# The inner X levels of a blocked triangular inversion: PSUM transposes of Y in place of a second set of small products

## The reference, cut to what matters

```
def _wkv7_step(S, inp):
    r, w, k, v, kk, a = inp
    sa = jnp.einsum('bhvk,bhk->bhv', S, kk)
    S = S * w[:, :, None, :] - sa[..., None] * (kk * a)[:, :, None, :] + v[..., None] * k[:, :, None, :]
    y = jnp.einsum('bhvk,bhk->bhv', S, r)
    return S, y
```

## Time and profile before

| | |
|---|---|
| runs | 2608.56, 2600.13, 2608.91 us; median 2608.56 |
| profiled execution | span 2600.0 us from first to last instruction; no whole time of its own is listed beside it |
| PE busy over the span | 2505.0 us (96%) |
| DVE, ACT busy over the span | 1998.4 us (77%), 1537.2 us (59%) |
| scan, 562 to 796 us | 234 us of the span (9%) |
| mean granted TensorE clock | 0.979 of 2.4 GHz |

### The profile page before, as it was taken

The page is one execution under the profiler, slowest core; times in us unless marked ns, Lnnn a source line. Parts: engine busy times, 40 slices in busy tenths (PEclk is TensorE's granted clock), DMA queues, the critical chain, the costliest instruction groups (busy, mean ns, idle before and its releaser), DMA issues.

```text
span 2600.0 us, 54588 instructions
## 1 busy us (share of the span) xinstructions
PE 2505.0 (96%) x23472; PEld 2331.7 (90%) x23472; DVE 1998.4 (77%) x3066; ACT 1537.2 (59%) x2510; POOL 51.9 (2%) x57
## 2 busy tenths in 40 slices
PE   8999999989999999999999999999898899999999
PEld 8779998868887899999999999999897799998999
DVE  5555547775544799999999999999877788675884
ACT  4435434464432677777777777777666566564663
POOL 0001100000000000000000000000003000000000
PEclk9999999978999999999999999999999999998999
DMA  6223452300003599999999999999732255541453
GB/s 246 73 74 122 178 190 100 107 1 4 20 4 115 206 376 337 367 340 368 341 366 335 372 337 370 335 373 345 287 139 105 78 192 191 188 173 50 171 181 128
DMA packets 83257, 538.46 MB, mean 207 GB/s; under 512 B 9488, under 2 KB 9616, under 8 KB 38976
## 3 DMA queue, kind: packets, MB, share of 16 engines
q1 hardware_dynamic: 82368, 530.68, 55.2%
q0 software_dynamic: 640, 4.22, 0.4%
HBM read 533.81 MB, written 1.05 MB: 206 GB/s over the span
## 4 chain that ended last, share of the span: by engine, by line
PE 87%; DVE 7%; ACT 4%; issue 1%; DMA 1%; DVEq 0%; SPq 0%; PEldq 0%; ACTq 0%
PE ps L576 23%; PE ps L577 23%; PE ps L578 23%; PE ps L1469 2%; DVE sl L534 2%; PE ps L591 1%; PE ps L582 1%; PE ps L2000 1%; PE ps L1463 1%; PE ps L1447 1%; PE ps L1454 1%; DMA ring<-ws_d 1%; PE ps L2145 1%; PE ps L1425 1%; PE ps L819 1%
## 5 line engine op out<-in xcount | busy, mean ns | idle before, releaser
L2227 DVE TENSOR_TENSOR sl<-ring,sh 128x1024 fp32r<-128x1024 f32 x613 | 718.1, 1219 | 13.5 <-ACT sh L2185 10.6
L2185 ACT ACTIVATE sh<-ring 128x1024 fp32r<-128x1024 f32 x613 | 609.0, 1061 | 1.3 <-DVE xl L2070 1.3
L576 PE MATMUL ps<-sh,xh 128*128 128x256 f32 (+2 forms) x2012 | 568.0, 282 | 2.1 <-DVE sl L534 1.2
L578 PE MATMUL ps<-sh,xl 128*128 128x256 f32 (+2 forms) x2012 | 567.5, 282 | 0.0
L577 PE MATMUL ps<-sl,xh 128*128 128x256 f32 (+2 forms) x2012 | 567.0, 282 | 0.0
L576 PE MATMUL ps<-xh,sh 128*128 128x256 f32 (+2 forms) x1856 | 538.5, 290 | 22.8 <-DVE sl L534 12.7
L577 PE MATMUL ps<-xl,sh 128*128 128x256 f32 (+2 forms) x1856 | 531.2, 286 | 0.0
L578 PE MATMUL ps<-xh,sl 128*128 128x256 f32 (+2 forms) x1856 | 529.0, 285 | 0.0
L534 DVE TENSOR_TENSOR sl<-ring,sh 128x1024 fp32r<-128x1024 f32 (+1 forms) x341 | 401.0, 1201 | 74.6 <-ACT sh L527 74.3
L527 ACT ACTIVATE sh<-ring 128x1024 fp32r<-128x1024 f32 (+1 forms) x341 | 338.8, 1021 | 111.2 <-PE ps L578 102.8
L576 PEld LDWEIGHTS ps<-sh,xh 128*128 128x128 f32 x2012 | 377.8, 188 | 11.8 <-DVE sl L534 1.6
(11 more groups left out here) (555 smaller groups left out, 3861.1 us busy)
## 6 DMA issues: line engine op xcount, KB each, us to landing
ring<-ws_d SPq DMA_DIRECT2D x229, 1024.0 KB, 7.2
ring<-ws_d SPq DMA_DIRECT2D x80, 1536.0 KB, 6.4
ring<-ws_d SPq DMA_DIRECT2D x225, 512.0 KB, 6.5
ring<-ws_d SPq DMA_DIRECT2D x24, 1408.0 KB, 6.0
ring<-ws_d SPq DMA_DIRECT2D x4, 1256.0 KB, 5.4
ring<-ws_d SPq DMA_DIRECT2D x2, 1088.0 KB, 5.0
scan_t<-scn_d POOLq DMA_DIRECT2D x1, 1844.0 KB, 7.5
ring<-ws_d SPq DMA_DIRECT2D x1, 1248.0 KB, 5.6
```

The source lines that it names most:

```text
L576: e.matmul(out, ah, bh, start=start, stop=False)
L578: return e.matmul(out, al, bh, start=False, stop=stop)
L2185: e.activation(out, raw(u)[:, a:z], ACT.Copy).then_inc(*af.on("high", u, i))
L2227: e.tensor_tensor(l, raw(u)[:, a:z], f32(h), SUB).then_inc(s_fd if i < 2 else s_fp, 1)
```

## The change

The change is that X of the levels 1 to 4 (1 and 2 in the small chunk) is no longer made by 16 products of its own. After T of the next level PE turns the whole of Y with four transposes of 128x128 into one PSUM bank, and DVE copies that bank, 128x512, over X. Y of every level and X of the last level stay products. For the transposes to give X in place, the slots of the heads in Y and X are renumbered.

```
         def g_slot(i, p):
             return 8 * (i // 2 % 2) + 4 * p + 2 * (i // 4) + i % 2
 
+        def x_slot(i):
+            return 2 * (i % 4) + i // 4
+
         def y_slot(i, p):
-            return 4 * p + i % 4
+            return 2 * (i % 4) + p
...
                         last.then_inc(*pe.on("T", *u, lv))
+                        if lv > 1:
+                            b, free = psum.take(("X turn", *u, lv - 1))
+                            w.wait_ge(*free)
+                            for k in range(4):
+                                last = tr(e, PS[:, b, 128 * k:128 * k + 128], d.Y[:, 2 * k:2 * k + 2, :].rearrange("q i t -> q (i t)"))
+                            last.then_inc(*pe.on("X turn", *u, lv - 1))
                         yield
                         w.wait_ge(ac["T", *u, lv], dv["X", *u, lv - 1])
                         if lv < levels(cn) - 1:
...
-                        b, free = psum.take(("X", *u, lv), 2)
-                        w.wait_ge(*free)
-                        for i, p in HEADS:
-                            last = e.matmul(spread(PS[own(p), b:b + 2, :], lv)[:, i], d.T[own(p, cn), i, :], side(d.X[own(p, cn), i, :], lv, d.x_side), start=True, stop=True)
-                        last.then_inc(*pe.on("X", *u, lv))
+                        else:
+                            b, free = psum.take(("X", *u, lv), 2)
+                            w.wait_ge(*free)
+                            for i, p in HEADS:
+                                last = e.matmul(spread(PS[own(p), b:b + 2, :], lv)[:, x_slot(i)], d.T[own(p, cn), i, :], side(d.X[own(p, cn), x_slot(i), :], lv, d.x_side), start=True, stop=True)
+                            last.then_inc(*pe.on("X", *u, lv))
...
                     for lv in range(1, levels(cn)):
+                        if lv > 1:
+                            w.wait_ge(pe["X turn", *u, lv - 1])
+                            e.tensor_copy(d.X.rearrange("q i t -> q (i t)"), PS[:, psum["X turn", *u, lv - 1], :]).then_inc(*dv.on("X", *u, lv - 1))
+                            psum.gone["X turn", *u, lv - 1] = [dv.now()]
                         yield
                         if lv < levels(cn) - 1:
                             b = psum["Y", *u, lv]
                             w.wait_ge(pe["Y", *u, lv])
-                            e.copy_predicated(side(d.Y, lv, d.y_side), level_mask(d.y_level, lv, d.y_side), spread(PS[:, b:b + 2, :], lv)).then_inc(*dv.on("Y", *u, lv))
+                            by_slot = PS[:, b:b + 2, :].rearrange("q p (i t) -> q i p t", i=4)[:, :, :, 0:32]
+                            e.copy_predicated(side(d.Y, lv, d.y_side), level_mask(d.y_level, lv, d.y_side), by_slot).then_inc(*dv.on("Y", *u, lv))
                             psum.gone["Y", *u, lv] = [dv.now()]
-                        w.wait_ge(pe["X", *u, lv])
+                        else:
+                            w.wait_ge(pe["X", *u, lv])
```

More of the change, by code:

```diff
@@ L1462, in steps @@
                             for i, p in HEADS:
-                                last = e.matmul(spread(PS[part(0, i), b:b + 2, :], lv)[:, y_slot(i, p)], d.X[own(p, cn), i, :],
+                                last = e.matmul(spread(PS[part(0, i), b:b + 2, :], lv)[:, 4 * p + i % 4], d.X[own(p, cn), x_slot(i), :],
                                                 side(d.T[own(p, cn), i, :], lv, d.y_side), start=True, stop=True)
                             last.then_inc(*pe.on("Y", *u, lv))
-                        b, free = psum.take(("X", *u, lv), 2)
-                        w.wait_ge(*free)
-                        for i, p in HEADS:
-                            last = e.matmul(spread(PS[own(p), b:b + 2, :], lv)[:, i], d.T[own(p, cn), i, :], side(d.X[own(p, cn), i, :], lv, d.x_side), start=True, stop=True)
-                        last.then_inc(*pe.on("X", *u, lv))
+                        else:
[4 more added lines that the diff above has]
+                            last.then_inc(*pe.on("X", *u, lv))
                         yield
@@ L1488, in steps @@
                     for i, p in HEADS:
-                        last = e.matmul(PS[part(0, i), b + p, col(i)], d.X[own(p, cn), i, :], d.Z[own(p, cn), i, :], start=True, stop=True)
+                        last = e.matmul(PS[part(0, i), b + p, col(i)], d.X[own(p, cn), x_slot(i), :], d.Z[own(p, cn), i, :], start=True, stop=True)
                     last.then_inc(*pe.on("N", *u))
@@ L1712, in steps @@
                     m = sn(f"{d.y_level}0")[:, 0:cn].bitcast(u32)
[L1713 removed]
+                    e.copy_predicated(d.Y[:, :, 0:cn].rearrange("q (i p) t -> q p i t", p=2), m[:, None, None, :].broadcast_to([128, 2, 4, cn]), eights(b, cn)).then_inc(*dv.on("Y", *u, 0))
                     psum.gone["Ut", *u] = [dv.now()]
@@ L1719, in steps @@
                             k = g_slot(4 * x, p)
-                            e.copy_predicated(d.X[own(p), 4 * x:4 * x + 4, d.x_side:cn:2].rearrange("s (q i) t -> s q i t", q=2), m[own(x)], g[own(x), :, k:k + 2, d.x_side:cn:2]).then_inc(*dv.on())
+                            e.copy_predicated(d.X[own(p), x::2, d.x_side:cn:2].rearrange("s (q i) t -> s q i t", q=2), m[own(x)], g[own(x), :, k:k + 2, d.x_side:cn:2]).then_inc(*dv.on())
                     dv.mark("X", *u, 0)
@@ L1727, in steps @@
                             w.wait_ge(pe["Y", *u, lv])
-                            e.copy_predicated(side(d.Y, lv, d.y_side), level_mask(d.y_level, lv, d.y_side), spread(PS[:, b:b + 2, :], lv)).then_inc(*dv.on("Y", *u, lv))
+                            by_slot = PS[:, b:b + 2, :].rearrange("q p (i t) -> q i p t", i=4)[:, :, :, 0:32]
+                            e.copy_predicated(side(d.Y, lv, d.y_side), level_mask(d.y_level, lv, d.y_side), by_slot).then_inc(*dv.on("Y", *u, lv))
                             psum.gone["Y", *u, lv] = [dv.now()]
-                        w.wait_ge(pe["X", *u, lv])
-                        b = psum["X", *u, lv]
-                        e.copy_predicated(side(d.X, lv, d.x_side), level_mask(d.x_level, lv, d.x_side), spread(PS[:, b:b + 2, :], lv)).then_inc(*dv.on("X", *u, lv))
-                        psum.gone["X", *u, lv] = [dv.now()]
+                        else:
+                            w.wait_ge(pe["X", *u, lv])
+                            b = psum["X", *u, lv]
+                            e.copy_predicated(side(d.X, lv, d.x_side), level_mask(d.x_level, lv, d.x_side), spread(PS[:, b:b + 2, :], lv)).then_inc(*dv.on("X", *u, lv))
+                            psum.gone["X", *u, lv] = [dv.now()]
                         yield
```

## The result

| | before | after |
|---|---|---|
| median of 7 runs each, us | 2608.56 | 2594.01 |
| range, us | 2600.13 to 2610.72 | 2587.75 to 2597.58 |
| span of the profiled execution, us | 2600.0 | 2592.2 |
| PE busy, us (records) | 2505.0 (23472) | 2495.7 (22520) |
| DVE busy, us | 1998.4 | 2003.7 |

The ratio is 0.9946, 95% interval 0.9931 to 0.9961. I had forecast 2613 in a range of 2598 to 2625. A second set of ten runs of the kernel after gave 2594.08, ratio 0.9953 (0.9938 to 0.9968). One execution of the kernel before, in the last series, took 10412.75 us and is left out of every comparison.

What follows compares the result with a forecast made beforehand. PE's own time was taken to bound the kernel, with instruction supply behind its broken groups. PE work +7.8, waits +2.3, end +1.2 and idles -6.8 gave +4.5 us on the median 2608.56: 2613 us, range 2598 to 2625.

Steps and rivals of the forecast that it cites:

- PE work added: In the scan, 34 turns of four transposes at 1.16 us each would add 39.4 us on PE.
- The change of shape: Around each turn in the scan, switching array tile size would cost 0.32 us: 0.11 on entering, 0.21 on leaving.
- PE work removed: In the scan, 34 groups of 16 X products at 0.93 us each go: 31.6 us less on PE.
- PE work: In the scan, products removed and turns added together would give +7.8 us, bounds -3.1 and +18.7.
- Idles that go: From 621 to 762 us, PE idles put down to instruction shortage would vanish: -6.8 us, bounds 0 and -10.
- Waits that come: In the scan, new PE waits for ACT and DVE where no fillers stand, 700 to 762 us: +2.3 us.
- the end: At the last level of stream 0, alone then, X would wait for turn and copy: +1.2 us.
- both sides double: At the halved clock, 586 to 621 us, PE work removed and added both double, changing the sum by about 1 us at most.
- rival 1: Instruction supply is the whole bound from 621 to 762 us, gaps shrink with the record count: -7, 2601 us; chance 0.25.
- The second (idles stay): PE's idles in the scan have a cause other than code fetching and remain: +11.3, 2620 us; chance 0.15.
- the third (double price of shape): Around each turn the small arrays empty on both sides, twice the 0.32 us: +15.4, 2624 us; chance 0.10.

Runs made afterwards that it cites:

- before plus a turn: The kernel before, all its products kept, with four unused transposes of Y behind T at levels 2 to 5, 34 times; ratio 1.0076.
- four tiles: The kernel after with fourteen one-column products of 64x64 ahead of T at 34 steps, spread over T's four 64x64 tiles; ratio 1.0035.

## Why the prediction was wrong

In the means over all executions the change is -12.7 us: **-10.2 at full clock and -2.5 of clock.** The first has an interval of 1.4 either way; the second one of 2.5, so it may be nothing.

- **The step that failed: "PE work added".** I took "eight records in place of 32" of the earlier trace rows for four transposes and put a turn at 0.84 + 0.32 = 1.16 us, 34 of them at 39.4. Measured, a turn is 0.50 (added to before) and 0.49 (taken from after): 17 us. The term was mis-sized by 22 us. Of these, 34 x (0.84 - 0.43) = 14 is the reading, shown by the turn made of products and by the doubled turn. The change of shape is 0.27 in the trace against 0.32, 2 us. The last 34 x (0.70 - 0.50) = 7 is length in the trace that does not show in the time. When a turn is added to the kernel after or taken from it, the waits behind DVE and ACT shrink and grow to match; for the turn added to before they do not, and there it stays open.
- *PE work removed*: -31.6 forecast; fourteen of sixteen products measured at -27.7 give -31.7 for sixteen, with what idles and waits changed along with them. Right as far as that tells. PE work is so 17 - 31.7 = -14.7, where I had +7.8.
- *Idles that go*: -6.8 forecast from the starved groups. They went: 5.6 us before, none listed after, in 620 to 750, and twice. Why is not shown. That PE ran out of instructions is what I took it for, and the records per us fit in three kernels (29.3, 28.2 and 26.8 with 5.6, 3.3 and 0 us); but before plus a turn has 26.6 (6798 in 255.3) with 2.8 us, one idle of 1.8 among them, and four tiles 28.2 (6661 in 236.3) with 1.1. The Trainium skill ("Runtime: NRT & Kernel Launch", Instruction fetch mechanics) has fetching hidden; no run here shows that these idles are fetching, nor that they are not. What they are worth in the time no run takes by itself: giving the 952 records back brought only 2.2 us of them with it.
- *Waits that come* and *the end*: +3.5 forecast. What is left between -14.7 and -10.2 is +4.5 for waits, end and idles together, where I had -3.3; it is good to some 3 us. The lists have the waits over the scan at +7.7 (10.3 to 18.0 in the means of two profiles each) and the idles at -6.0, so of the two it is the waits that I had too small. *The end* came out at +0.9 for the +1.2: from T's start to X's of the last level 2.13 us (776.17 to 778.30), 1.26 before (786.67 to 787.93). The largest new wait has a cause that I overlooked; it is told below the list.
- *The clock* had no term in my sum. I said that both sides double at the halved clock; what I missed is that the time at half clock changes with the kernel: the clock took 50 to 73 us over the kernels, a spread nearly as wide as my range of 27. For the kernel itself it is 2.5 of the 12.7.
- *The rivals*: the first (supply the whole bound, 2601) was nearest in size and wrong in cause. The second (idles stay) is refuted by the lists, the third (double price of shape) by the 0.27. My check in the text, "under 1.0 rival 1", pointed at the right row; the cause of 0.59 was the record count.

The new wait that I overlooked: I let S's wait for N shrink by 0.5 a round; it grew, to 2.4 us of the 6.4 in 620 to 750 (line 1510). That line (1500 before), which I had called the first half of S, is in the kernel's text the part of y that comes from the old state, and it doesn't read N. It waits for its PSUM banks. They are given out so:

```
    def take(self, key, n=1):
        b = self.turn
        if b % n or b + n > 8:
            b = -(-b // n) * n % 8
        self.turn = (b + n) % 8
        ...
```

Before, N, T, S and y take two banks each, all eight. After, the turn takes one between T and S, S moves up to the next even bank, and y comes round to the two banks of N, which are free only when ACT has copied N. In before, and in before without the X products, line 1500 never waits for ACT; with the turn left out but its bank still taken, line 1510 waits 4.5 us. This is read from the kernel's text and the lists; no run gives the turn its bank in another way.

The Trainium skill ("TensorEngine Tiling (Array Packing)", Key Properties) says that a change of tile size drains the array. The traces agree, with 0.11 on entering (T takes 0.60 in place of 0.49) and 0.16 on leaving (0.59 less 0.43 of streaming).

Open: what sets the granted clock in the scan. It comes again with the kernel and moves by up to 17 us between kernels whose full-clock lengths are within 4 us (67.3 with four tiles, 50.0 with the turn by products). PE's busy share doesn't explain it, and full-width products in the idle time raised it only where they stood. Open too: what the idles without a waiter are.

## What to carry to other kernels

Before a duration is divided by a count, find how many records one instruction leaves: here an fp32 product two, a transpose of the same size one, so a row of x8 was eight transposes and I read four; the loops of the line behind the row say the same. A full-width transpose of 128x128 costs 0.105 us, a group of sixteen 64x64 products 0.5 to 0.9, so replacing a result that is another's transpose paid here, 0.5% of the kernel. Where buffers are handed out in rotation, ask also whose buffer each later step now comes round to. And where a kernel touches the halved clock, compare spans times clock beside times: an edit may gain 10 us of work and the clock give or take as much.

## What the runs showed of the hardware

- An fp32 transpose of 128x128 takes about half of an fp32 product of that size: four more transposes lengthen a turn by 0.43 us, and making its four as products lengthens it by 0.50 (1.09 against 0.59).
- A product of one column is not cheap: fourteen took 0.91 us on two of the small arrays and added 0.40 to 0.47 on four, hardly under the 0.49 of T's sixteen with 32 columns.
- The granted clock differs by kernel in a repeatable way: it took 66.6 and 67.7 us in two series with the X copy doubled, 58.9 and 56.8 in two series of the kernel after, 58.5 to 60.9 in four of before. The two kernels with longer turns, one series each, have 51.3 and 50.0.
